# Sample outputs moved one sample ahead of the prompt's head pairs, table loads moved ahead of the near scores, and the two halves of a w_o column tile loaded in the other order

## The reference, cut to what matters

```python
z = rms_norm(x) @ w_in                       # q | k | v | u, 2048 -> 4096 columns
# prompt: causal, three (window, dilation) branches, merged by their denominators
# samples: the same over cache_k / cache_v (2048 rows) and the new rows
attn = merge([dilated(q, k, v, bias, d, w // d) for (w, d) in ((128, 1), (512, 4), (2048, 16))])
pool = per_group_linear(window_means(u) - u) * pool_scale   # 4 groups x 256
x = x + concat(attn, pool) @ w_o             # 2048 x 2048
x = x + hier_moe(rms_norm(x))                # 1 of 4 groups, 2 of 4 experts in it
```

## Time and profile before

| | us |
|---|---|
| median of 3 runs | 1006.85 (1006.47 to 1006.91) |
| the profiled execution's own time | 1008.58 |
| its span, first to last instruction | 1006.80 |
| TensorE busy | 918.8 (91%) |
| VectorE busy | 289.0 (29%) |
| ScalarE busy | 125.7 (12%) |
| bytes moved | 339.18 MB, 337 GB/s in the mean |

### The profile page before, as it was taken

One profiled execution on the slowest core, in us unless ns is written; L12 is line 12 of the kernel. 1 busy time (PEld: TensorE's weight loads), 2 busy tenths in 40 slices (PEclk: granted clock), 3 DMA queues, 4 the chain that ended last, 5 costly groups with the idle time before them and its releaser, 6 DMA issues.

```text
span 1006.8 us, 10088 instructions
## 1 busy us (share of the span) xinstructions
PE 918.8 (91%) x4351; PEld 448.1 (45%) x4351; DVE 289.0 (29%) x411; ACT 125.7 (12%) x285; POOL 46.8 (5%) x85
## 2 busy tenths in 40 slices
PE   9999999999989979999959999988899688997884
PEld 5444444444345657777743334332343234432331
DVE  1127999992443420111151101110011101101001
ACT  4200111211034520000010000001010010000000
POOL 0003001011010000000010000000000000000000
PEclk9999999999999989999969999999999999999998
DMA  9956799983969974557288999999999999999991
GB/s 332 395 199 229 290 403 374 351 330 101 355 231 401 402 274 181 190 213 320 109 313 342 389 404 421 422 422 421 421 422 420 422 422 421 421 422 422 421 391 58
DMA packets 81570, 339.18 MB, mean 337 GB/s; under 512 B 7605, under 2 KB 11679, under 8 KB 57281
## 3 DMA queue, kind: packets, MB, share of 16 engines
q1 hardware_dynamic: 61503, 296.45, 73.9%
q10 hardware_dynamic: 16096, 33.84, 9.0%
q0 software_dynamic: 3920, 8.19, 2.4%
HBM read 329.71 MB, written 12.24 MB: 340 GB/s over the span
## 4 chain that ended last, share of the span: by engine, by line
PE 71%; DMA 24%; DVE 2%; issue 1%; ACT 0%; SPq 0%; POOL 0%; ACTq 0%; POOLq 0%; DVEq 0%
PE PS L885 67%; DMA ring<-in_w_up 10%; DMA ring<-in_w_gate 4%; DMA ring<-in_w_down 2%; DMA aux<-in_w_up 2%; DMA aux<-in_w_down 2%; DMA X<-in_cache_k 1%; DMA ring<-in_cache_v 1%; PE PS L972 1%; PE PS L906 1%; DMA X<-x_scr,pidx 1%; PE PS L1214 1%; DMA eye<-in_c_eye 1%; PE PS L1125 0%; DVE Z L1855 0%
## 5 line engine op out<-in xcount | busy, mean ns | idle before, releaser
L885 PE MATMUL PS<-ring,HT 128*128 128x512 f32 (+2 forms) x1184 | 370.2, 600 | 9.0 <-DMA ring<-in_w_up 6.6
L885 PE MATMUL PS<-ring,Z 128*64 128x512 f32 (+2 forms) x912 | 240.5, 590 | 25.0 <-DMA ring<-in_w_up 8.7
L885 PEld LDWEIGHTS PS<-ring,HT 128*128 128x128 f32 (+2 forms) x1184 | 140.2, 156 | 201.6 <-issue 200.6
L885 PEld LDWEIGHTS PS<-ring,Z 128*64 128x64 f32 (+1 forms) x912 | 83.4, 142 | 147.3 <-issue 142.1
L885 PE MATMUL PS<-HT,ring 128*128 128x288 f32 x512 | 129.5, 412 | 5.7 <-issue 5.7
L885 PEld LDWEIGHTS PS<-HT,ring 128*128 128x128 f32 x512 | 97.3, 193 | 33.0 <-issue 7.3
L885 PE MATMUL PS<-aux,Z 128*64 128x512 f32 (+2 forms) x208 | 73.2, 533 | 3.7 <-ACT aux L820 1.4
L885 PE MATMUL PS<-Z,X 128*128 128x256 f32 x128 | 42.1, 463 | 10.5 <-DMA X<-x_scr,pidx 4.8
L1915 DVE TENSOR_TENSOR Z<-Z,PS 128x512 f32<-128x512 f32 x8 | 5.5, 688 | 146.6 <-PE PS L885 146.6
L1855 DVE TENSOR_TENSOR Z<-PS,ln2R 128x512 f32<-128x512 f32 x16 | 11.1, 692 | 121.9 <-PE PS L885 121.9
L885 PEld LDWEIGHTS PS<-Z,X 128*128 128x128 f32 x128 | 33.2, 326 | 27.2 <-issue 13.0
(11 more groups left out here) (216 smaller groups left out, 526.6 us busy)
## 6 DMA issues: line engine op xcount, KB each, us to landing
ring<-in_w_gate SPq DMA_DIRECT2D x27, 2048.0 KB, 21.5
ring<-in_w_up SPq DMA_DIRECT2D x25, 2048.0 KB, 22.2
ring<-in_w_down SPq DMA_DIRECT2D x23, 2048.0 KB, 22.5
ring<-in_w_in ACTq DMA_DIRECT2D x12, 2048.0 KB, 17.2
ring<-in_w_o SPq DMA_DIRECT2D x8, 2048.0 KB, 11.8
ring<-in_cache_v SPq DMA_DIRECT2D x8, 1536.0 KB, 8.7
ring<-in_cache_v SPq DMA_DIRECT2D x32, 384.0 KB, 9.3
aux<-in_w_gate SPq DMA_DIRECT2D x5, 2048.0 KB, 25.0
```

Of the source, the lines that this page charges most:

```text
L885: return pe.matmul(out, lhsT, rhs, start=start, stop=stop, skip_group_check=True)
```

## The change

TensorE computes the outputs of sample 0 ahead of the loop, before it turns the heads of pair 0, and in turn i the outputs of sample i + 1. The copies on ScalarE (`sample_outputs_out`) and VectorE (`sample_outputs_in`) move by the same step. On SP the loads of `state`, `c_pool`, `wpool` and the bias table `T` go ahead of the reload of the near scores. The first w_o column tile is loaded half 1 first. On VectorE `fold_samples(7)` goes behind the whole softmax, and the zeroing of bank 4 no longer waits for the last projected column. The end of the loop is ordered anew on TensorE: five instead of four blocks of w_o ahead of the rest, and the rest of pooling and of pair 7 spread between the other blocks. The chunks before are multiplied in the order 8 to 11, 12, 13, 0 to 6, 14, 7, 15, with `group_map(5)` and the turns of pair 7 ahead of them all; after, in the order 8 to 12, 0 to 6, 13, 14, 7, 15, with `group_map(5)` behind 12, the turn of pair 7's probabilities behind 1, `prompt_outputs(7)` and `group_map(6)` behind 3, and `group_map(7)` behind 13. `sample_outputs_in(b)` is the pair of copies to `hT` that stood at the end of VectorE's turn, as a function of the sample.

```diff
@@ sync (SP)
             keys(n)
+        sp.wait_ge(k_used, 2 * DEC_B - 1)
+        sp.dma_start(state, ...).then_inc(state_in, 16)
+        sp.wait_ge(k_used, 2 * DEC_B)
+        sp.dma_start(c_pool, a["c_pool"]).then_inc(pool_in, 16)
+        sp.dma_start(wpool, ...).then_inc(pool_in, 16)
         sp.wait_ge(g_stored, 16)
+        sp.dma_start(T, ...).then_inc(T_in, 16)
         for n in range(2):
             sp.wait_ge(near_out[n], 16 * 4 * DEC_B // 2)
         sp.dma_start(Pf[:, 0:512], near_scr).then_inc(near_back, 16)
...
-        sp.wait_ge(k_used, 2 * DEC_B - 1)
-        sp.dma_start(state, ...).then_inc(state_in, 16)
-        sp.wait_ge(k_used, 2 * DEC_B)
-        sp.dma_start(c_pool, a["c_pool"]).then_inc(pool_in, 16)
-        sp.dma_start(wpool, ...).then_inc(pool_in, 16)
-        sp.wait_ge(g_stored, 16)
-        sp.dma_start(T, ...).then_inc(T_in, 16)
         for b in range(2):
             sp.wait_ge(half_used, 7 + b)
...
         sp.wait_ge(o_done, DEC_B - 1)
-        load_columns(sp, w_o_t, 0, 0)
+        load_half(sp, w_o_t, 0, 0, 1)
+        load_half(sp, w_o_t, 0, 0, 0)
@@ scalar (ACT)
+        def sample_outputs_out(b):
+            act.wait_ge(o_done, b + 1)
+            act.wait_ge(sOT, b)
+            act.activation(OS, PS[:, 4, 0:256], ACT.Copy).then_inc(os_moved, 1)
+        sample_outputs_out(0)
         heads_turned(0)
         for i in range(PAIRS):
...
             if i + 1 < PAIRS:
                 heads_turned(i + 1)
-            act.wait_ge(o_done, i + 1)
-            act.wait_ge(sOT, i)
-            act.activation(OS, PS[:, 4, 0:256], ACT.Copy).then_inc(os_moved, 1)
+                sample_outputs_out(i + 1)
@@ tensor (PE)
+        pe.wait_ge(ptm_moved, 3)
+        pe.wait_ge(ptn_moved, 1)
+        pe.wait_ge(o_zero, 1)
+        pe.wait_ge(vn_in, 80)
+        pe.wait_ge(v_in[0], 96)
+        outputs(0, (6, 0, 1, 2, 7, 3, 4, 5)).then_inc(o_done, 1)
         pe.wait_ge(z_moved, 16)
         pe.wait_ge(fold_done, 8)
...
+        turn_sample_outputs(0)
         head_scores(0)
         for i in range(PAIRS):
             windows(i)
-            pe.wait_ge(v_in[i % 2], 96 * (i // 2 + 1))
...
-            outputs(i, (6, 0, 1, 2))
+            b = i + 1
+            if b < DEC_B:
+                pe.wait_ge(v_in[b % 2], 96 * (b // 2 + 1))
+                pe.wait_ge(os_moved, b)
+                if i:
+                    pe.wait_ge(po_moved, i)
+                outputs(b, (6, 0, 1, 2))
                 turn_heads(i + 1)
-            outputs(i, (7, 3, 4, 5)).then_inc(o_done, 1)
+                outputs(b, (7, 3, 4, 5)).then_inc(o_done, 1)
                 head_scores(i + 1)
                 turn_prompt_probs(i)
                 if i >= 2:
                     group_map(i - 2)
-                turn_sample_outputs(i)
+                turn_sample_outputs(b)
                 prompt_outputs(i)
...
-        group_map(5)
-        turn_prompt_probs(7)
-        turn_sample_outputs(7)
         pe.wait_ge(qk_moved, 2 * PAIRS)
         pe.wait_ge(landed[1], 16 * (BASE_WO[1] + 1))
         pe.wait_ge(y_moved, 5)
-        for k in range(4):
+        for k in range(5):
             first_block(8 + k, start=k == 0)
+        group_map(5)
+        pe.wait_ge(landed[0], 16 * (BASE_WO[0] + 1))
+        pe.wait_ge(ot_moved, DEC_B)
+        pe.wait_ge(po_moved, PAIRS - 1)
+        for i in range(2):
+            first_block(i)
+        turn_prompt_probs(7)
+        for i in range(2, 4):
+            first_block(i)
         prompt_outputs(7)
         group_map(6)
...
@@ vector (DVE)
-        fold_samples(7)
         dve.wait_ge(sm_exp, 1)
...
             dve.tensor_tensor(by_step(Pf, n), by_step(Pf, n), wide4(n), ALU.mult).then_inc(sm_norm, 1)
+        fold_samples(7)
...
-        dve.wait_ge(z_moved, 16)
         dve.memset(PS[:, 4, 0:256], 0.0).then_inc(o_zero, 1)
         dve.wait_ge(T_in, 32)
+        sample_outputs_in(0)
         for i in range(PAIRS):
...
+            if i + 1 < DEC_B:
+                sample_outputs_in(i + 1)
```

More of the change, by code:

```diff
@@ L425, in _ @@
             keys(n)
+        sp.wait_ge(k_used, 2 * DEC_B - 1)
+        sp.dma_start(state, a["state_pool"][0].rearrange("b r n -> (b r) n")).then_inc(state_in, 16)
+        sp.wait_ge(k_used, 2 * DEC_B)
+        sp.dma_start(c_pool, a["c_pool"]).then_inc(pool_in, 16)
+        sp.dma_start(wpool, a["w_pool"][0].rearrange("g (c p) e -> p g c e", p=P)).then_inc(pool_in, 16)
         sp.wait_ge(g_stored, 16)
+        sp.dma_start(T, bass.AP(g_scr.tensor, 0, [[1, P], [384, H], [1, 256]])).then_inc(T_in, 16)
         for n in range(2):
@@ L439, in values @@
             far_rows(sp, "cache_v", b, v_tile[n][:, 3:6, :], v_in[n])
-        sp.wait_ge(k_used, 2 * DEC_B - 1)
-        sp.dma_start(state, a["state_pool"][0].rearrange("b r n -> (b r) n")).then_inc(state_in, 16)
-        sp.wait_ge(k_used, 2 * DEC_B)
-        sp.dma_start(c_pool, a["c_pool"]).then_inc(pool_in, 16)
-        sp.dma_start(wpool, a["w_pool"][0].rearrange("g (c p) e -> p g c e", p=P)).then_inc(pool_in, 16)
-        sp.wait_ge(g_stored, 16)
-        sp.dma_start(T, bass.AP(g_scr.tensor, 0, [[1, P], [384, H], [1, 256]])).then_inc(T_in, 16)
         for b in range(2):
@@ L1144, in prompt_outputs @@
             ins.then_inc(pO, 1)
+        pe.wait_ge(ptm_moved, 3)
[4 more added lines that the diff above has]
+        outputs(0, (6, 0, 1, 2, 7, 3, 4, 5)).then_inc(o_done, 1)
         pe.wait_ge(z_moved, 16)
         pe.wait_ge(fold_done, 8)
-        pe.wait_ge(ptm_moved, 3)
         pe.wait_ge(normed, 4)
@@ L1155, in _ @@
             windows(i)
[L1156 to L1159, removed]
-            pe.wait_ge(v_in[i % 2], 96 * (i // 2 + 1))
-            if i:
-                pe.wait_ge(os_moved, i)
-                pe.wait_ge(po_moved, i)
-            outputs(i, (6, 0, 1, 2))
-            if i + 1 < PAIRS:
+            b = i + 1
[5 more added lines that the diff above has]
+                outputs(b, (6, 0, 1, 2))
                 turn_heads(i + 1)
-            outputs(i, (7, 3, 4, 5)).then_inc(o_done, 1)
-            if i + 1 < PAIRS:
+                outputs(b, (7, 3, 4, 5)).then_inc(o_done, 1)
                 head_scores(i + 1)
@@ L1187, in _ @@
         pe.wait_ge(y_moved, 5)
-        for k in range(4):
+        for k in range(5):
             first_block(8 + k, start=k == 0)
+        group_map(5)
[7 more added lines that the diff above has]
+            first_block(i)
         prompt_outputs(7)
         group_map(6)
-        first_block(12)
+        for i in range(4, PAIRS - 1):
+            first_block(i)
         first_block(13)
[L1194 to L1197, removed]
         group_map(7)
-        for i in range(3, PAIRS - 1):
-            first_block(i)
         first_block(14)
@@ L1655, in _, with sample_outputs_in @@
                               own.unsqueeze(1).to_broadcast([P, ns * P, 4]), ALU.mult).then_inc(ptm_moved, 1)
-        dve.wait_ge(z_moved, 16)
         dve.memset(PS[:, 4, 0:256], 0.0).then_inc(o_zero, 1)
         dve.wait_ge(T_in, 32)
+        def sample_outputs_in(b):
+            dve.wait_ge(sOT, b + 1)
+            for e in range(2):
+                r = slice(64 * e, 64 * e + 64)
+                blocks = PS[r, 5, 4 * e:4 * e + 272].rearrange("p (c x) -> p c x", x=136)[:, :, 0:128].rearrange(
+                    "p c (s y) -> p s c y", y=32)[:, :, :, 0:4]
+                ins = dve.tensor_copy(hT[r, 0:PAIRS, SEQ + 4 * b:SEQ + 4 * b + 4].rearrange(
+                    "p (s c) t -> p s c t", c=2), blocks)
+                if e == 0:
+                    did(ins)
+            ins.then_inc(ot_moved, 1)
+        sample_outputs_in(0)
         for i in range(PAIRS):
```

## The result

The changed kernel takes 999.39 us (median of 4 runs, 998.65 to 1000.76); the kernel before, run beside it, 1006.66 (4 runs, 1005.18 to 1006.91). The ratio is 0.9926, with an interval of 0.9907 to 0.9944: 7.3 us, 0.7%, faster. The forecast was 997.4 in a range of 995.0 to 1001.2. The profiled execution took 1000.76, its span is 999.0 (before: 1008.58 and 1006.8).

The account below looks back on a forecast made before the run. Expert weight transfers bound 600 to 980 us, but start from a TensorE event, so time saved before 500 us reaches the end. Terms 1.25 - 0.4 - 0.4 + 5.71 + 3.2 = 9.4 off 1006.85 gave 997.4, range 995.0 to 1001.2.

Parts of the forecast that it names:

- The wait for w_o, 5.71: Ahead of TensorE's first w_o products: loading half 1 first removes the wait, gaining 5.71 us, bounds 4.2 and 5.71.
- The clock, 3.2: At the first w_o products: without the wait TensorE's clock does not fall, gaining 3.2 us, bounds 0 and 3.2.
- The rival that the clock falls all the same: At the wait ahead of outputs(0) or transfer stops: clock falls anyway, gain 6.2 us, so 1000.6; chance 0.08.
- The softmax, 1.25: Fold moved behind the softmax: TensorE's wait ahead of the first turn of probabilities goes, gaining 1.25 us.
- The tables, 0: Four loads on SP moved ahead of the near scores: no gain alone, 0 us, bounds 0 to -1.
- The slower rival: Table load delays the near scores' return, so all samples' softmax starts late: kernel slower, 1011.6 us at 32 us; chance 0.04.
- The entry, -0.4: At the loop's entry: 2.1 us of waits against 1.68 before, a loss of 0.4 us, bounds 0 and -1.
- The loop, -0.4: In the sample loop: a wait of 1.1 us at sample 2 against 0.69, a loss of 0.4, bounds +0.7 and -2.
- rival B: Sample loads bind the loop: outputs(7) 3.5 us later than forecast, gain 5.9, so 1001.0 us; chance 0.16.
- rival D: At the end: the expert stream's start hangs on something else, nothing arrives, time stays 1006.9 us; chance 0.04.

Follow-up runs that it names:

- Run 1: Kernel before with only the two w_o halves reordered, half 1 loaded first: 999.62 us against 1006.63, ratio 0.9932.
- run 4: Changed kernel with the two w_o halves back in the old order: 1001.1 us, ratio 0.995.
- run 12: Kernel before with only half 1 of w_o loaded first, measured again on another chip: 1001.48 us, ratio 0.9941.
- Run 8: Kernel before with 12 matmuls into a bank nothing reads, ahead of the kept wait for half 1 of w_o: 1005.39 us, ratio 0.9974.
- run 2: Kernel before with 24 matmuls into a bank nothing reads, ahead of the kept wait for half 1 of w_o: 1012.16 us, ratio 1.0052.
- run 5: Changed kernel with the near value rows of samples 0 and 1 loaded earlier, into another part of the same buffer: 1000.37 us, ratio 0.992.
- run 7: Changed kernel with state, c_pool, w_pool and the table loaded at their old place behind the near scores: 999.17 us, ratio 0.9915.
- run 11: Changed kernel measured again, unaltered, on another chip: 1000.21 us, ratio 0.9932.
- run 3: Kernel before with only the fold of the last samples' columns moved behind the softmax: 1005.63 us, ratio 0.9993.
- run 9: Kernel before with only half 1 of w_o loaded first and the fold behind the softmax: 999.35 us against 1008.37, ratio 0.992.
- run 6: The kernel of run 5 with ScalarE also copying PTn ahead of the last columns' second copy-out: 998.64 us, ratio 0.9896.
- run 10: The kernel of run 6 with 17 matmuls nobody reads ahead of four routing waits: 997.31 us against 1008.37, ratio 0.9894.

## Why the prediction was right, and where it was off

**The wait for w_o, 5.71: right.** The forecast had the halves landing at 355 and 360.5; they landed at 355.2 and near 360.5. Run 1 shows that the order of the halves is enough, run 4 that without it 1.45 stay.

**The clock, 3.2: right.** The first w_o matmuls, `prompt_outputs(7)` and `group_map(6)` stand in the same order before and in run 12. They take 6.95 us before, up to the row below, and 3.92 at the upper level in run 12 (361.32 to 365.24): 3.0 less. Run 8 gives 3.05, and the sum above leaves 2.82.

```profile
373.41 2.59 PE L885 MATMUL PS<-HT,ring 128*128 128x288 f32 x10
```

The rival that the clock falls all the same did not come in this profile, at the wait of 1.78 either. The argument against it was weaker than it looked: waits of 0.78 and 0.90 at the loop's entry left the clock at 1.00 before, but it fell right behind the same two waits in runs 1, 2 and 12. In runs 2 and 12 that cost 1.57 us (5.41 against 3.84). The forecast was made against a profile that happened to have no such fall. The profiles of the changed kernel and of runs 4, 5, 7 and 11 have none there, which is too few to call it a gain of the change.

**The softmax, 1.25: right**, 1.47 here; the fold is hidden as forecast, and VectorE waits for ScalarE's exponentials (timeline of the changed kernel):

```profile
259.21 0.69 DVE L1643 TENSOR_TENSOR aux<-PS,aux 128x512 f32<-128x512 f32 x1 [24.76 <-PE PS L1026]
...
266.75 1.37 ACT L786 ACTIVATE aux<-aux 128x1408 f32<-128x1408 f32 x1
268.15 2.40 DVE L1652 TENSOR_REDUCE stat<-aux 128x4 f32<-128x512 f32 x4 [3.85 <-ACT aux L786]
...
273.31 0.73 DVE L1546 TENSOR_SCALAR aux<-PS,stat 32x512 f32<-32x512 f32 x1
```

**The tables, 0: right** (run 7). The slower rival fell with it: in the changed kernel VectorE's add of the near scores at 259.21 (first row above) waits for TensorE's scores, not for their transfer.

**The entry, -0.4: right**, 2.12 against 1.68.

**The loop, -0.4: this step failed in size.** It was -1.72, inside its bounds of +0.7 and -2. The forecast put one wait of 1.1 at sample 2, where its landing at 304 was right (304.38). It took the 2.1 MB of sample 1 for landed at 293.4; TensorE stood for them until 294.64. And it let turns run on without a wait behind sample 2, where 0.54 came at sample 4. The step weighed how much earlier the stream starts, and not how much earlier its first consumer comes. Sample 1 is wanted 6.4 us earlier (at 293.57 after, 299.96 before), since sample 0 starts 4.6 us earlier and the prompt's probabilities and outputs of pair 0 no longer stand between the two. But its last five transfers go out only 2.0 us earlier: at 284.78, against this row of before.

```profile
286.80 0.35 SPq L344 DMA_DIRECT2D ring<-in_cache_v  x1
```

For sample 2 both moved by 5.3 us, so it had no more time than before, behind a queue that was fuller. The windows of the changed kernel show the queue full from 288 us on, where before its share in the first of these windows was 0.78. Only what goes out ahead of that relieves it, as in run 5, whose stretch was 1.0 us shorter:

```profile
288.00:300.00 12.00, 10.59 (x143) 6.07 (x133) 3.79 (x10) 4.36 (x15) 2.40 (x5) 1.00 1.00 370
300.00:320.00 20.00, 17.84 (x210) 11.24 (x209) 7.58 (x20) 9.42 (x29) 0.00 (x0) 1.00 1.02 403
320.00:350.00 30.00, 29.46 (x331) 18.76 (x329) 12.83 (x35) 15.86 (x48) 0.00 (x0) 1.00 1.02 399
```

That is rival B in part: the loads bind in three turns, by 2.4 us, 1.3 more than the forecast had, where the rival asked for 3.5 more. `outputs(7)` start at 350.28, not at 353. The rival's figure from the Trainium skill (DMA: Bandwidth & Descriptors, Specifications), about 358 GB/s from HBM for a core, is not what sets it: these windows move 399 to 403.

How firm is that term? The waits for samples differ from profile to profile of the same loop. In the old order they are 0.7, 2.5, 0, 1.3, 1.3, 0.2 and 2.1 us (before, runs 1, 2, 3, 8, 9, 12), 1.2 in the mean; in the new order, with the loads as in the change, 2.4, 2.1, 2.2 and 2.3 (after, runs 4, 7, 11). (In runs 1, 2 and 12 the fall of the clock at the entry also delays the consumer.) So the 0.69 that I took for the kernel before was one draw, and run 9's 0.17 a good one. The reordered loop costs about 1.1 us more in such waits, and 0.4 at the entry. What it brings is w_o some 2.6 us earlier (345.61 against 348.18 in run 9), and with the halves in the new order that saves no more than the waits of 0.20 and 0.24 in run 9. It pays with the old order of the halves (144.63 in run 4, 148.82 in run 3). That the change would be faster without it is what the stretches say (141.35 and 143.25 on one chip, one profile each; with the old order's mean wait run 9 would come to some 142.4, an estimate). The times (ratios 0.992 and 0.9932) don't tell the two apart, so it is not shown.

**The sum.** Forecast 1.25 - 0.4 - 0.4 + 5.71 + 3.2 = 9.4; measured in the stretch 1.47 - 0.44 - 1.72 + 5.71 + 2.82 = 7.84, the 2.82 being what is left over. The stretch's gain carries to the end, as forecast, and rival D is refuted: the lead is 8.40 us at the end of w_o, 7.89 where TensorE starts on the gathered tokens (512.59 against 520.48). Behind that it depends on where the clock falls, in this timeline and these windows of the changed kernel:

```profile
512.59 6.32 PE L890 MATMUL PS<-Z,X 128*128 128x256 f32 x20 [4.77 <-DMA X<-x_scr,pidx]
```
```profile
540.00:542.00 2.00, 2.00 (x6) 0.48 (x4) 0.00 (x0) 1.97 (x3) 0.18 (x1) 0.50 0.99 418
542.00:544.00 2.00, 2.00 (x10) 0.68 (x8) 0.00 (x0) 0.02 (x1) 0.00 (x0) 0.75 1.03 434
```

The selection is 1.2 us shorter than before (6.32 against 7.52), and a fall at 540 us that the profile of before does not have takes it back; runs 4 and 7, with the same instructions there, have no such fall. The two go together in all 14 profiles. Where the selection took 7.3 to 7.7 us (before, runs 2, 4, 7, 8) the clock stays up behind it; where it took 4.8 to 7.1 (the other nine) it falls once more between 536 and 548 us. So a shorter selection did not carry to the end in full; why it is so was not tried. The rest, from 7.8 between the profiles to 7.3 between the medians, lies within the spread of the runs and is not settled.

## What to carry to other kernels

When two transfers go out together, ask which one the consumer touches first; two lines of order were worth about 7 us in the medians here (runs 1 and 12). Before moving a consumer forward, compare how far its loads move with it: where the transfer of one turn is as long as the turn, slack lost at the start comes back as waits. And price an idle wait together with the clock behind it: the wait at w_o cost 5.7 us, and some 3 more after it was over.

## What the runs showed of the hardware

- The clock's fall is not a matter of one wait's length alone. After a wait of 1.78 us at 286.53 the 32 matmuls took 1.92 us; after 1.60 in run 1, 1.87 in run 6 and 2.31 in run 10 the same 32 took 3.43, 3.30 and 3.57. Waits of 0.78 and 0.90 at the loop's entry were followed by a granted clock of 1.00 before and in runs 3, 8 and 9, and by 0.50 to 0.56 (window 288 to 290) in runs 1, 2 and 12. What decides between these was not tried.
- Two transfers of 2 MB on one queue, issued together, land one after the other: 10.6 and 15.6 us before, 9.6 and 14.4 after, 10.5 and 15.4 in run 9. The second takes 5 us more, so in these runs which goes first is worth about 5 us to whoever waits.
- A float32 product stands as two rows in the trace: 24 products of 264 columns in run 2 as 48 rows, 0.45 us a product at the upper level.
